# More early expert scores, in split products, in a fused transformer kernel on Trainium2

## The reference, cut to what matters

```python
def peer_ffn(xn, wq, subkeys, u_tab, v_tab):        # xn: 256 x 1024, u_tab, v_tab: 16384 x 1024
    q = (xn @ wq).reshape(b, s, 8, 2, 128)
    sc = jnp.einsum('bshjc,hjkc->bshjk', q, subkeys)         # 16 lists of 128 scores for each token
    top_s, top_i = lax.top_k(sc, 16)
    cand = (top_s[..., 0, :, None] + top_s[..., 1, None, :]).reshape(b, s, 8, 256)
    best, ci = lax.top_k(cand, 16)
    i1 = take_along_axis(top_i[..., 0, :], ci // 16);  i2 = take_along_axis(top_i[..., 1, :], ci % 16)
    idx = i1 * 128 + i2
    g = jax.nn.softmax(best, axis=-1)
    ...
    act = gelu(einsum('ckd,cd->ck', u_tab[idx], x))
    return einsum('ck,ckd->cd', g * act, v_tab[idx])
```

## Time and profile before

| | us |
|---|---|
| median of 3 runs | 3377.08 (3373.78 to 3378.36) |
| profiled execution, whole | 3372.12 |
| its span | 3370.6 |
| PE busy | 3150.4 (93%) |
| DVE busy | 1972.9 (59%) |
| ACT busy | 1586.5 (47%) |
| POOL busy | 274.8 (8%) |

### The profile page before, as it was taken

How to read it: one execution, slowest core, us unless ns; L and a number is a source line. 1 busy time by engine, 2 the same in 40 slices (tenths; PEclk the granted TensorE clock), 3 DMA queues, 4 the chain that set the end, 5 groups by cost and what they waited for, 6 DMA issues and landing times.

```text
span 3370.6 us, 49973 instructions
## 1 busy us (share of the span) xinstructions
PE 3150.4 (93%) x18836; PEld 2673.9 (79%) x18836; DVE 1972.9 (59%) x4121; ACT 1586.5 (47%) x3320; POOL 274.8 (8%) x376
## 2 busy tenths in 40 slices
PE   6998999998899978997999999998899789999999
PEld 3745677776699867986789999988788678999998
DVE  3233433335666556689666666656659876666665
ACT  2254322223655425319555555542541765555554
POOL 0021000000200021008000000001200620000000
PEclk9999999998999988999999999999799999999999
DMA  6502444432155423440455556543144035555554
GB/s 227 178 1 76 156 175 161 166 105 94 45 170 180 156 73 103 152 144 1 157 187 187 186 185 200 182 162 110 56 162 152 30 113 182 187 188 187 184 186 150
DMA packets 135052, 479.82 MB, mean 142 GB/s; under 512 B 15520, under 2 KB 17440, under 8 KB 134048
## 3 DMA queue, kind: packets, MB, share of 16 engines
q1 hardware_dynamic: 132944, 471.26, 42.6%
q10 hardware_dynamic: 1872, 5.38, 0.4%
HBM read 475.53 MB, written 1.05 MB: 141 GB/s over the span
## 4 chain that ended last, share of the span: by engine, by line
PE 88%; DVE 5%; ACT 3%; issue 2%; DMA 1%; POOL 0%; SPq 0%; DVEq 0%; ACTq 0%; POOLq 0%
PE psum L768 15%; PE psum L770 15%; PE psum L769 15%; PE psum L2941 7%; PE psum L2943 7%; PE psum L2942 7%; PE psum L2850 7%; PE psum L2759 4%; PE psum L863 2%; PE psum L1125 2%; PE psum L356 1%; PE psum L1135 1%; PE psum L629 1%; DMA raw<-in_mod_w 1%; DVE a_scaled L733 1%
## 5 line engine op out<-in xcount | busy, mean ns | idle before, releaser
L249 DVE TENSOR_TENSOR w_lo<-raw,w_hi 128x512 fp32r<-128x512 f32 x1424 | 958.4, 691 | 744.9 <-ACT w_hi L240 717.6
L240 ACT ACTIVATE w_hi<-raw 128x512 fp32r<-128x512 f32 x1424 | 864.4, 625 | 795.7 <-PE psum L770 419.3
L768 PE MATMUL psum<-x_hi,w_hi 128*128 128x256 f32 x1968 | 561.2, 285 | 7.7 <-issue 4.2
L770 PE MATMUL psum<-x_hi,w_lo 128*128 128x256 f32 x1968 | 558.2, 284 | 0.0
L769 PE MATMUL psum<-x_lo,w_hi 128*128 128x256 f32 x1968 | 557.7, 283 | 0.0
L2941 PE MATMUL psum<-w_hi,wt_hi 128*128 128x512 f32 x1024 | 406.9, 397 | 6.5 <-DVE wt_lo L3005 6.5
L2943 PE MATMUL psum<-w_hi,wt_lo 128*128 128x512 f32 x1024 | 406.4, 397 | 0.0
L2942 PE MATMUL psum<-w_lo,wt_hi 128*128 128x512 f32 x1024 | 405.8, 396 | 0.0
L768 PEld LDWEIGHTS psum<-x_hi,w_hi 128*128 128x128 f32 x1968 | 373.5, 190 | 17.6 <-issue 9.0
L769 PEld LDWEIGHTS psum<-x_lo,w_hi 128*128 128x128 f32 x1968 | 376.1, 191 | 7.9
L770 PEld LDWEIGHTS psum<-x_hi,w_lo 128*128 128x128 f32 x1968 | 375.1, 191 | 0.0
(11 more groups left out here) (336 smaller groups left out, 4439.0 us busy)
## 6 DMA issues: line engine op xcount, KB each, us to landing
raw<-in_v SPq DMA_DIRECT2D x256, 512.0 KB, 4.4
raw<-in_u SPq DMA_DIRECT2D x190, 512.0 KB, 3.4
raw<-in_mod_w SPq DMA_DIRECT2D x96, 512.0 KB, 4.4
raw<-in_w_gate_up SPq DMA_DIRECT2D x88, 512.0 KB, 5.2
u_raw<-in_u SPq DMA_DIRECT2D x66, 512.0 KB, 3.5
raw<-in_w_in SPq DMA_DIRECT2D x40, 512.0 KB, 3.5
raw<-in_w_down SPq DMA_DIRECT2D x32, 512.0 KB, 3.5
raw<-in_w_peer SPq DMA_DIRECT2D x32, 512.0 KB, 4.2
```

The lines of the kernel that those rows point to most:

```text
L240: self.nc.scalar.activation(self.hi[:, m % 4, :], self.half(m), ACT.Copy).then_inc(self.rounded[m % 4], 1)
L249: self.nc.vector.tensor_tensor(self.lo[:, m % 4, :], self.half(m), self.hi[:, m % 4, :], ALU.subtract).then_inc(self.ready[m % 4], 1)
L768: pe.matmul(out[:, 0:width], hi[:, w], x_hi, start=(c == 0), stop=False)
L770: mm = pe.matmul(out[:, 0:width], lo[:, w], x_hi, start=False, stop=(c == total - 1))
```

## The change

EARLY goes from 33 to 41. Of the 41 early tiles the first two stay plain; 39 are computed in split products. For those, ACT rounds the two halves of a tile into `u_hi`, GpSimd subtracts them into `u_lo` (VectorE does the same for all other weights), and TensorE runs 24 matmuls of 256 columns with the already split `x_hi` and `x_lo`. The load of a raw tile now waits for GpSimd's subtraction of three tiles before. ACT's Gelu comes two tiles behind the rounding. In the routing, the longest operations with two operands in SBUF get one of them from PSUM: `places` is read from `numbers` in bank 4, `top_f` lies in bank 5, and the second half of `top` is copied to bank 5 (`others`) ahead of the sums. The matmul for `numbers` moves ahead of the early scores. The `Experts` have 87 scores left to make instead of 95, and `rowbuf` lies in the last 8 tiles of `early`.

```diff
-EARLY = 33
+EARLY = 41
 class Route:
+        self.held = k.bank[5].use(written=0)
+        self.top_f = self.held.tensor[:, 0:256].rearrange("p (n k) -> p n k", n=16)
+        self.others = self.held.tensor[:, 256:384].rearrange("p (h k) -> p h k", h=PEER_H)
-        self.top_f = k.sb("top_f", [P, 16, TOPK], 141824)
...
-        places = self.iota[:, 0:TOPK].unsqueeze(1).unsqueeze(1).to_broadcast(full)
+        places = self.numbers.tensor[:, 0:TOPK].unsqueeze(1).unsqueeze(1).to_broadcast(full)
...
-        hold(v, self.iota_done)
+        v.wait_ge(*self.held.free())
+        v.wait_ge(*self.numbers.full())
...
-            v.wait_ge(*k.vstep(v.tensor_copy(self.top_f[:], self.top_i[:])))
+            k.vstep(v.tensor_copy(self.top_f, self.top_i[:]))
+            v.wait_ge(*k.vstep(v.tensor_copy(self.others, halves_[:, :, 1, :])))
             v.wait_ge(*k.vstep(v.tensor_tensor(self.cand[:], halves_[:, :, 0, :].unsqueeze(3).to_broadcast(full),
-                                               halves_[:, :, 1, :].unsqueeze(2).to_broadcast(full), ALU.add)))
+                                               self.others.unsqueeze(2).to_broadcast(full), ALU.add)))
 class EarlyScores:
+    PLAIN = 2
     def sync(self):
-            if t >= 3:
+            if 3 <= t < 3 + self.PLAIN:
                 sp.wait_ge(*self.uses[t - 3].full())
+            elif t >= 3:
+                sp.wait_ge(*self.rest.after(self.halves_done(t - 3, 2)))
     def tensor(self):
             for c in range(DC):
+                w, out = slice(c * P, (c + 1) * P), use.tensor[:, 0:LAT]
+                if t < self.PLAIN:
+                    m = pe.matmul(out, self.raw[:, t % 3, w], self.xn[:, c, :], start=(c == 0), stop=(c == DC - 1))
+                    continue
+                if c % 4 == 0:
+                    pe.wait_ge(*self.rest.after(self.halves_done(t, c // 4 + 1)))
+                hi, lo = self.hi[:, t % 3, w], self.lo[:, t % 3, w]
+                pe.matmul(out, hi, self.x_hi[:, c, :], start=(c == 0), stop=False)
+                pe.matmul(out, hi, self.x_lo[:, c, :], start=False, stop=False)
+                m = pe.matmul(out, lo, self.x_hi[:, c, :], start=False, stop=(c == DC - 1))
     def scalar(self):
+        for t in range(EARLY + 2):
+            if self.PLAIN <= t < EARLY:
+                act.wait_ge(*self.there(t))
+                if t >= 3:
+                    act.wait_ge(*self.uses[t - 3].full())
+                for h in range(2):
+                    act.activation(self.half(self.hi, t, h), self.half(self.raw, t, h),
+                                   ACT.Copy).then_inc(self.rounded.sem, 1)
+            if t >= 2:
+                use = self.uses[t - 2]
+                act.wait_ge(*use.full())
+                act.activation(self.early[:, t - 2, :], use.tensor[:, 0:LAT], ACT.Gelu).then_inc(use.read.sem, 1)
+    def gpsimd(self):
+        pool = self.k.nc.gpsimd
+        for t in range(self.PLAIN, EARLY):
+            for h in range(2):
+                pool.wait_ge(*self.rounded.after(self.halves_done(t, h + 1)))
+                pool.tensor_tensor(self.half(self.lo, t, h), self.half(self.raw, t, h), self.half(self.hi, t, h),
+                                   ALU.subtract).then_inc(self.rest.sem, 1)
 class Peer:
     def tensor(self):
+        pe.wait_ge(*self.numbers.free())
+        pe.matmul(self.numbers.tensor[:, 0:P], self.k.ident, self.iota[:], start=True,
+                  stop=True).then_inc(self.numbers.written.sem, 1)
         self.scored.tensor()
-        self.gate.tensor_numbers()
```

## The result

| | before | after |
|---|---|---|
| median of the timed runs, us | 3375.43 (3372.26 to 3378.36, 4 runs) | 3334.13 (3328.73 to 3340.34, 4 runs) |
| ratio | | 0.9875, 95% interval 0.9857 to 0.9893 |
| span of the profiled execution | 3370.6 | 3327.4 |
| whole profiled execution | 3372.12 | 3328.73 |

The account below looks back on a forecast made before the run. TensorE was taken to bound the kernel: -22.7 (late scores) + 5.65 (early) = -17.1 us a layer, -34.2 in all, so 3377.1 - 34.2 = 3343 us. Forecast range 3336 to 3352; with most of two rivals, 3334 to 3362.

Parts of the forecast that it names:

- The gates: Gates stage: VectorE's L2801 about +0.03 us, ACT's L2822 about -0.03; taken as 0, bounds -2 and +2 us.
- the start: Start of the early scores, pipe of loads empty: bounds 0 and 2 us, taken as 0.
- The level before: Whole kernel before the change: median 3377.1 us, 5.0 above the profiled execution, from which 34.2 was subtracted.
- What bounds the kernel; early and late scores: TensorE, 88% of the chain; a layer's early scores +5.65 us, eight late scores -22.7, net -17.1.
- ACT, loads and start: Early scores: ACT's 1.62 of 2.88 us a tile and the loads cost nothing; start taken as 0.
- the prediction's own sign: Prediction is wrong if TensorE waits in the early scores, or VectorE's end comes behind ACT's last Gelu.
- GpSimd's price: Early scores: 78 subtractions a layer at 1.27 us, 99.1 of 112.3 us; below 1.44 each TensorE stays the bound.
- The rival of a dearer form: GpSimd's early subtractions set the pace from 1.44 us; at 1.55, +8.6 us a layer, 3360 us; chance 0.08.
- The routing: VectorE beside the early scores: 112 us, bounds 106 and 119, ending at 1507 before the scores at 1513.9.
- The rival "the routing outlasts the scores": Early stage: ten short VectorE operations each wait for two of GpSimd's, 25 us in both layers, 3368 us; chance 0.06.
- The slower rival, searches that collide with GpSimd: Early stage: routing's searches and GpSimd exclude each other, stage 204 us, 170 us more in both layers, 3513; chance 0.06.
- The rival "more than reckoned": The gates gain a few us instead of standing still, 3338 us; chance 0.04.

Follow-up runs that it names:

- second execution: The changed kernel, unchanged, measured once more with five rounds against the kernel before: 3337.98 us, ratio 0.9882.

## Why the prediction had the mechanism right and the size wrong

The mechanism was forecast: TensorE bounds both stages, three other engines keep up with a tile every 2.88 us, and the gain is that of the cheaper early scores. What failed is the sum that gives the time. It came to 3343 us and 3334.1 were measured, 8.9 less, and they come from three places:
- *The gates were taken at 0.* They gave 1.7 and 0.8 us, 2.5 of the 3.0 us by which the two layers beat the forecast (0.9 and 1.6 in the second execution). This is the term of the change that was mis-sized, and the step that failed; it is taken up below.
- *Code that the change does not touch was given no spread.* The prediction widened its forecast by the start and the gates only, -4 to +8 us by their own bounds, which is 3339 to 3351 (it wrote 3336 to 3352 without a source for the rest). About 4 us of the difference are of this kind: the mark `sc` came 6.0 us earlier in the profile of after and 5.8 us later in its second execution, and the medians of the same kernel are 3334.1 and 3338.0.
- *The level before* was the median of three executions, 3377.1. With a fourth it was 3375.4, 1.7 us of the 8.9, and later sets of 8 and 14 gave 3373.0 and 3374.4.

So that the measured time stands at the very edge of the range is the gates and, for the larger part, spread. The term by term account follows.

**What bounds the kernel; early and late scores.** Right. TensorE's early stage was to grow by 5.65 us a layer and grew by 5.95 and 5.6; the last two early Gelus stand 2.87 us apart (1505.34 to 1508.21), 2.88 was taken from the queries. The eight late scores were to bring 22.7 us a layer. The marks give 23.15 twice, but these hold unchanged code too: from the table load to the last matmul of the experts it is 22.1 and 24.0, and 21.9 and 22.9 in the second execution. A full step takes 5.660, 5.673 or 5.680 us, mostly the same through a whole stage, and that differs between executions of the same kernel (layer 1: 5.660 and 5.673); over 87 steps 0.013 are 1.1 us. Within that the term was right; what sets the step's length is open. The steps with `v` alone still take 2.81 us, and there are 41 of them now:

```profile
1717.30 0.42 ACT L3022 ACTIVATE wt_hi<-early 128x256 fp32r<-128x256 f32 x1 [0.71 <-PE psum L2989]
1720.11 0.42 ACT L3022 ACTIVATE wt_hi<-early 128x256 fp32r<-128x256 f32 x1 [0.72 <-PE psum L2989]
```

**ACT, loads and start.** Right. ACT waited 7.9 us for loads, six times, without making TensorE late. Taken at 0 within bounds of 0 and 2: the stage was 0.3 us longer than its sum in layer 0, and none in layer 1. By the letter of the prediction's own sign (wrong if TensorE waits in the early scores) the 0.3 us of waiting count against it; they cost nothing that shows.

**GpSimd's price.** Right: 1.27 us taken, 1.30 measured, 1.42 at most, all under 1.44. The rival of a dearer form fell with it. The single line after (ns minimum, median, maximum):

```profile
L2904 POOL TENSOR_TENSOR u_lo<-u_raw,u_hi x156: 1264/1301/1417, 1391.0 to 2598.6; 128x512 fp32r<-128x512 f32 x156
```

**The routing.** Right, and slightly too dear. From its first instruction at 1389.1 to the end of the last reduction at 1499.0 it took 109.9 us (112 forecast, 105.1 before), and ended 9 us before the last Gelu. (The prediction has the scores of before end at 1507.8; the earlier trace rows give 1394.23 + 113.98 = 1508.21. No term hangs on it.) VectorE in order of time:

```profile
1427.12 1.32 DVE L2688 TENSOR_SCALAR part_i<-best_i 128x128 uint32<-128x128 uint32 x1
1428.47 0.23 DVE L2689 CAST part_f<-part_i 128x128 f32<-128x128 uint32 x1
...
1496.70 2.29 DVE L2694 TENSOR_REDUCE res<-pick 128x128 f32<-128x2048 f32 x1
```

Short integer operations and two-operand ones in SBUF (0.21 and 0.29 us alone) do wait, for one subtraction of GpSimd: four of the six in layer 0 took 1.16 to 1.32 us, the other two their 0.21 and 0.29. The casts behind them took 0.23, but each of them starts in a gap of GpSimd; in the run with the operands in SBUF three of the four took 1.22. Operations of 2048 elements with one operand in PSUM take 2.29 as before. So an operand in PSUM costs them nothing: 2.293 us before, 2.287 after (bounds -0.01 and +0.06). The rival "the routing outlasts the scores" fell.

**The slower rival, searches that collide with GpSimd,** fell by the groups of the early stage after (busy us, mean ns):

```profile
L2657 DVE MATCH_REPLACE8 rest<-top,sc 128x128 f32<-128x128 f32 x32 | 8.4, 276 | 0.0
L2660 DVE MAX8 top<-rest 128x8 f32<-128x128 f32 x32 | 6.4, 277 | 0.1
L2663 DVE FIND_INDEX8 top_i<-top,rest 128x8 uint32<-128x128 f32 x32 | 8.4, 285 | 0.0
```

In the kernel before, with GpSimd idle, they take 276, 276 and 284 ns.

**The gates: the step that failed.** The prediction took them at 0 within -2 and +2 and priced each edit at 0.03 us. The measured sizes are 0.057 on either engine, 1.8 ns an element on VectorE and not 0.7, and the net is -1.7 and -0.8 us a layer. The 0.7 was drawn through two instructions of different kinds (multiplication from PSUM with a strided operand; subtraction in SBUF). The sentence "both engines set the pace" was right, but it was not worked into two loops: one price was set against the other and they were taken to cancel. In the trace of before only ACT's loop of 2.84 us is closed and VectorE's 2.68 has room. With that, even the prediction's own 0.03 us would have given 32 x 0.03 = 1.0 us a layer; the measured prices give the 1.6, because VectorE's loop then becomes the longer one. The gates are 2.5 of the 3.0 us by which the layers beat the forecast; by the marks the late scores are 0.9 and the early ones -0.3, both within their spread. The rival "more than reckoned", at 0.04, was what happened.

**The remaining 4 us of the first measurement** came from no step of the sum: the median of four executions differs by that much between two sets of the same kernel (3334.1 and 3338.0), and in the profiles the difference lies mostly in stretches that the change does not touch.

## What to carry to other kernels

When one engine is the bound of a stage and others stand idle beside it, price the work by the idle engine's own row, even if that engine is twice as slow: the threshold is the bound's period (here 1.44 us a subtraction), and what is under it is free as long as its neighbours have room. Look first at what the moved work shares with its neighbour: here operands moved from SBUF to PSUM kept VectorE and GpSimd out of each other's way, for less than 1 us of copies a layer. And when two engines both stand near 94% in a stage, write down each one's loop and its length; the stage goes by the longer one, and an edit pays only if it shortens that one, and only down to the other. And compare stages from a mark on, not whole times, when the difference looked for is a few microseconds: code that nobody touched moved by up to 12.

## What was not expected of the hardware

With the routing's operands in SBUF, VectorE's subtraction of 128 elements at L2685 took 6.01 us (1434.60 to 1440.61) where it takes 0.29 alone. GpSimd in the same stretch of that kernel, and the single line L2685 (ns minimum, median, maximum):

```profile
1417.02 23.44 POOL L2904 TENSOR_TENSOR u_lo<-u_raw,u_hi 128x512 fp32r<-128x512 f32 x17
```

```profile
L2685 DVE TENSOR_TENSOR res<-best x4: 1257/3666/6008, 1434.6 to 2608.9; 128x128 f32<-128x128 f32 x4
```

It ended when GpSimd's unbroken row of 17 subtractions ended, at 1440.46, and so seems to have been passed over by four of them, while the cast and the sums in front of it and the comparison just behind it waited for one. In layer 1 the same instruction took 5.98 us, again until GpSimd's row ended. The Trainium skill ("SBUF — State Buffer", Who interferes with whom) calls the pair of ports that the two engines share an exclusive lock, says that a VectorE instruction with two inputs in SBUF contends with a GpSimd instruction that reads SBUF, and that the order of issue decides who waits. The wait for one instruction agrees with that; a wait through several is more than the page tells. In the kernel after the same instruction took 1.13 us by the median and 1.16 at most, so a GpSimd without gaps is part of it, but no run here took this apart, and its cause is open. What it would mean for the change: two such waits a layer would have used up the 9 us by which the routing ends early.
